# Six of the second layer's projections as seven block products each, over tokens that are normalized before they are turned

## The reference, cut to what matters

```python
def rmsnorm(x, g):
    y = xf * lax.rsqrt(jnp.mean(xf * xf, axis=-1, keepdims=True) + RMS_EPS)
    return (y * g.astype(jnp.float32)).astype(x.dtype)
...
    kv = (rmsnorm(x, g_kv) @ w_kv).reshape(b, t, N_DIL, 2, N_KV_B, HEAD_DIM)
...
    q = rmsnorm((h @ w_q).reshape(b, t, N_DIL, N_HEADS_B, HEAD_DIM), q_norm[:, None, :])
```

## Time and profile before

| | |
|---|---|
| median of 3 executions | 1359.59 us (1357.63 to 1359.62) |
| the profiled execution, its own time | 1362.34 us |
| its span in the trace | 1360.5 us |
| mean granted TensorE clock | 0.981 of 2.4 GHz |
| busy share of the span | PE 94%, DVE 47%, POOL 36%, ACT 24% |

### The profile page before, as it was taken

How to read it: one execution, slowest core, us unless ns; L and a number is a source line. 1 busy time by engine, 2 the same in 40 slices (tenths; PEclk the granted TensorE clock), 3 DMA queues, 4 the chain that set the end, 5 groups by cost and what they waited for, 6 DMA issues and landing times. The chain is left out here.

```text
span 1360.5 us, 20795 instructions
## 1 busy us (share of the span) xinstructions
PE 1275.2 (94%) x8580; PEld 894.0 (66%) x8580; DVE 639.7 (47%) x1018; ACT 331.5 (24%) x667; POOL 495.3 (36%) x415
## 2 busy tenths in 40 slices
PE   8999999999999988899999999999998999997786
PEld 6787887546566654458877877877755666664443
DVE  3578775524522211173559559558436572221114
ACT  2223322302122222140115015015005312222112
POOL 4466744101111111016876576576450111111101
PEclk8999999999999999899999999999999989999899
DMA  8446635577799999961113012013050899999996
GB/s 310 140 141 220 220 122 197 189 309 279 315 417 418 418 418 420 376 244 59 52 56 97 9 55 97 9 56 97 9 140 6 344 357 418 418 419 419 419 419 265
DMA packets 92768, 318.82 MB, mean 234 GB/s; under 512 B 32969, under 2 KB 45401, under 8 KB 66564
## 3 DMA queue, kind: packets, MB, share of 16 engines
q1 hardware_dynamic: 77956, 279.95, 52.9%
q0 software_dynamic: 13536, 33.29, 6.9%
q10 hardware_dynamic: 1184, 4.26, 0.8%
HBM read 300.19 MB, written 33.28 MB: 245 GB/s over the span
## 5 line engine op out<-in xcount | busy, mean ns | idle before, releaser
L2069 PE MATMUL ps<-slots 128*128 128x384 f32 x768 | 262.0, 495 | 1.1 <-DVE vo L2368 0.7
L2069 PEld LDWEIGHTS ps<-slots 128*128 128x128 f32 x768 | 203.0, 270 | 43.9 <-issue 3.2
L1215 PE MATMUL ps<-slots,oT 128*64 128x256 f32 x1216 | 160.9, 398 | 23.5 <-DMA slots<-in_w_up 21.9
L1215 PEld LDWEIGHTS ps<-slots,oT 128*64 128x64 f32 x1216 | 108.4, 144 | 72.6 <-issue 24.9
L1241 DVE TENSOR_TENSOR sg<-sg,ps 64x256 f32<-64x256 f32 x64 | 26.4, 413 | 242.9 <-ACT sg L1238 242.9
L1727 POOL DMA_INDIRECT xs<-xn_rows,idx x30 | 30.7, 1024 | 238.8 <-PE ps L1204 166.5
L1733 POOL DMA_INDIRECT y_rows<-ysb,idx x30 | 30.1, 1005 | 172.4 <-DVE ysb L1250 172.4
L1238 ACT ACTIVATE sg<-ps 64x256 f32<-64x256 f32 x64 | 24.4, 381 | 237.1 <-PE ps L1215 237.1
L1250 DVE COPY ysb<-ps 64x512 f32<-64x512 f32 x60 | 41.6, 694 | 85.8 <-PE ps L1233 79.9
L602 PE MATMUL ps<-xnT_a,wA 128*128 128x260 f32 (+1 forms) x320 | 76.9, 397 | 1.5 <-DVE xnT_a L866 1.4
L1233 PE MATMUL ps<-slots,hT 128*64 128x512 f32 x320 | 74.0, 598 | 4.2 <-issue 4.2
(11 more groups left out here) (338 smaller groups left out, 2335.5 us busy)
## 6 DMA issues: line engine op xcount, KB each, us to landing
slots<-in_w_up SPq DMA_DIRECT2D x42, 1024.0 KB, 28.0
slots<-in_w_down SPq DMA_DIRECT2D x40, 1024.0 KB, 29.0
slots<-in_w_gate SPq DMA_DIRECT2D x34, 1024.0 KB, 25.9
slots<-in_unit_weights_b SPq DMA_DIRECT2D x12, 1536.0 KB, 6.8
wA<-in_qkv_pairs_a SPq DMA_DIRECT2D x24, 512.0 KB, 3.8
apart<-in_w_gate SPq DMA_DIRECT2D x10, 1024.0 KB, 28.0
spare<-in_w_gate SPq DMA_DIRECT2D x8, 1024.0 KB, 27.8
scratch<-in_w_gate SPq DMA_DIRECT2D x8, 1024.0 KB, 28.5
```

The lines of the kernel that those rows point to most:

```text
L1215: last = nc.tensor.matmul(bank(q)[lo:lo + CAP, 0:FE], x[:, k, :], wt[:, k, :], start=(k == 0), stop=(k == KT - 1))
L2069: last = nc.tensor.matmul(bank(i % 2)[:, 0:UW], xT[:, kt, cols], wB[:, g, kt, :], start=(kt == 0), stop=(kt == KT - 1))
```

## The change

Four things change in `layer_b`:

1. **Tokens normalized at their turn.** `turn_x` becomes a matmul of the same stationary `x` with a diagonal matrix of `rs` instead of a transpose with the identity. So a tile's squares and `rs` come first. ACT makes the diagonal, in `gain_rows`. Evictions no longer multiply, and `rsr` with its two transfers is gone.
2. **Six units as seven block products.** Units 4, 5, 7, 8, 10, 11 (groups 1 and 2 of key heads 1 to 3) split tokens (residues 0, 1 and 2, 3), depth (4 and 4 blocks of 128) and columns (192 and 192) in halves, and form seven products of the Winograd kind. A product is 8 matmuls, 128 by 128 stationary and 128 by 192 moving. DVE makes the mixed tokens once (`mix_tokens`, 4 instructions) and the mixed weights per unit (`mix_weights`, 4 instructions of 768 elements per partition with both inputs in SBUF), and combines the products in `evict_mixed`. The sample tokens are part 7, as before.
3. **Raw blocks copied gapless.** ACT copies the unmixed token blocks once to places where their columns are neighbours. The last unit's third part reads `xT` with the stride instead.
4. **Norm weights by ScalarE.** `scale` goes from DVE to ACT (16 instructions a unit) for all units but unit 1. The parts of unit (j+1, 1) are also written one step earlier than its chunks were.

```diff
             NSTEP, NPART = sum(STEPS), 8
+            UQ, UH, HK = UW // 4, UW // 2, KT // 2
+            PARTS = ((0, 1), (2, 3), (4, 5), (6,), (7,))
+            def mixed(n):
+                return n > NDIL and n % NDIL > 0
...
                     def turn_x(t, rows):
-                        pe.wait_ge(s_cb, 3 * t + 3)
+                        pe.wait_ge(s_dg, t + 1)
...
-                            last = nc.tensor.transpose(dst[:, kt, 0:rows], x[0:rows, t, kt:D:KT], ident[0:rows, 0:rows])
+                            last = nc.tensor.matmul(dst[:, kt, 0:rows], x[0:rows, t, kt:D:KT], diag[0:rows, t % 2, 0:rows], start=True, stop=True)
...
+                    def mixed_part(n, part):
+                        g, i, w = n % NDIL, chunk0[n] + part, wB[:, n % NDIL]
+                        lower = copies[1] if n < NDIL * NKV - 1 else x_res[:, HK:KT, 0:2]
...
+                        elif part in (1, 3, 5):
+                            pe.wait_ge(s_wm, mixed0[n] + (2, 3, 4)[part // 2])
+                        pe.wait_ge(s_ev, i - 1)
...
+                            tokens = (copies[0], mix_x[1], lower, mix_x[2], mix_x[0], None, mix_x[3])[part]
...
+                        act.wait_ge(s_cb, 3 * t + 3)
+                        norm.square(act, t, junk)
+                        if t == 0:
+                            scale(0, 1, range(KT - 3, KT)).then_inc(s_ws, 1)
+                        act.wait_ge(norm.s_rstd, t + 1)
+                        nc.scalar.activation(diag[0:rows, t % 2, 0:rows], ident[0:rows, 0:rows], ACT.Copy, scale=rs[0:rows, t:t + 1]).then_inc(s_dg, 1)
                         act.wait_ge(s_xt, t + 1)
...
-                        norm.square(act, t, junk)
...
+                        turned(j, 0)
+                        if j < NKV - 1:
+                            scale_unit(j + 1, 0)
+                            scale_unit(j + 1, 1)
+                        turned(j, 1)
+                        if j < NKV - 1:
+                            scale_unit(j + 1, 2)
+                        turned(j, 2)
...
+                    def evict_mixed(j, g, part):
...
+                        if part == 0:
+                            room(j, g)
+                            V.tensor_copy(first_p, got).then_inc(s_ev, 1)
+                        elif part in (1, 3):
+                            dve.wait_ge(s_ev, i)
+                            V.tensor_tensor(early if part == 1 else late, first_p, got, ALU.add).then_inc(s_ev, 1)
...
+                            out, one, other = ((t1, b12, b11), (t2, b22, t1), (t3, b22, b12), (t2, b21, t2))[step]
+                            V.tensor_tensor(out, one, other, ALU.subtract).then_inc(s_wm, 1)
...
+                        parts(0, 1)
+                        soft(j, 2, 0)
                         if more:
-                            scale(j + 1, 1)
-                        ahead(1, 4)
-                        soft(j, 2, 0)
+                            mix_weights(j + 1, 1, (3,))
                         ahead(2, 0)
+                        parts(2)
                         soft(j, 2, 1)
                         far_max(j)
                         ahead(2, 1)
+                        parts(3, 4)
```

More of the change, by code:

```diff
@@ L2056, in project @@
                         n = 3 * j + g
-                        i = NCHUNK * n + c
+                        if mixed(n):
+                            for part in PARTS[c]:
+                                mixed_part(n, part)
+                            return
+                        i = chunk0[n] + c
                         if c == 0:
@@ L2073, in project @@
                                 pe.wait_ge(s_xc, NT)
-                            for kt in range(KT):
-                                for q in range(4):
-                                    last = nc.tensor.matmul(bank(i % 2)[32 * q:32 * q + DEC, 0:UQ], xT[:, kt, SEQ:TOK],
-                                                            wB[:, g, kt, UQ * q:UQ * q + UQ], start=(kt == 0), stop=(kt == KT - 1))
+                            last = sample_rows(i, g)
+                        last.then_inc(s_proj, 1)
@@ L2196, in _, with parts @@
                     project(0, 0, 4)
-                    for c in range(NCHUNK):
+                    for c in range(NT):
                         project(0, 1, c)
                     for j in range(NKV):
+                        more = j < NKV - 1
+                        def parts(*which):
+                            for part in which if more else ():
+                                mixed_part(3 * j + 4, part)
                         def ahead(u, c):
@@ L2239, in _ @@
                         ahead(1, 3)
+                        if more:
+                            ahead(1, 4)
+                            parts(0)
                         turn_back(j, 2, 0)
@@ L2255, in _ @@
                         weigh(j, 1)
-                        ahead(2, 3)
+                        parts(6)
                         turn_p(j, 3)
@@ L2260, in _ @@
                         weigh(j, 3)
-                        ahead(2, 4)
+                        parts(7)
                         turn_p(j, 5)
@@ new lines, in mix_tokens @@
+                    def mix_tokens(step):
+                        x11, x12, x21, x22 = [x_res[:, HK * i:HK * i + HK, c:c + 2] for c in (0, 2) for i in range(2)]
+                        out, one, other, op = ((0, x21, x22, ALU.add), (2, x11, x21, ALU.subtract), (1, mix_x[0], x11, ALU.subtract),
+                                               (3, x12, mix_x[1], ALU.subtract))[step]
+                        if step == 0:
+                            dve.wait_ge(s_xc, 4)
+                        elif step > 1:
+                            dve.wait_ge(s_mix, (1, 3)[step - 2])
+                        V.tensor_tensor(mix_x[out], one, other, op).then_inc(s_mix, 1)
@@ L2478, in _ @@
                     scale(0, 1)
-                    for c in range(2, NCHUNK):
+                    for c in range(2, NT):
                         evict(0, 0, c)
-                    for c in range(NCHUNK):
+                        if c == 2:
+                            for step in range(4):
+                                mix_tokens(step)
+                    for c in range(NT):
                         evict(0, 1, c)
-                        if c == 1:
-                            scale(0, 2)
                     for j in range(NKV):
@@ L2494, in ahead, with parts @@
                             elif more:
-                                evict(j + 1, u - 1, c)
+                                if u == 1:
+                                    evict(j + 1, 0, c)
                             elif (u, c) in GIVEN:
                                 out_b.add(dve, 0, GIVEN[u, c], at=0)
-                        if more:
-                            scale(j + 1, 0)
+                        def parts(*which):
+                            for part in which if more else ():
+                                evict_mixed(j + 1, 1, part)
                         ahead(0, 0)
+                        if j:
+                            mix_weights(j, 2, (3,))
                         ahead(0, 1)
@@ L2538, in _ @@
                         if more:
[L2539 to L2540 removed]
+                            mix_weights(j + 1, 2, (0, 1, 2))
+                        parts(6)
                         p_copy(j, 3)
```

177 lines of the change are left out of this document (131 added, 46 removed).

## The result

| | before | after |
|---|---|---|
| median of 4 executions | 1358.61 us | 1383.51 us (1383.21 to 1384.06) |
| ratio, 95% interval | | 1.0188 (1.0169 to 1.0207) |
| profiled execution, its span | 1362.3, 1360.5 us | 1383.2, 1381.4 us |
| PE busy, mean granted clock | 94%, 0.981 | 92%, 0.979 |

The forecast had the sign, but 1368.3 was too little by 15 us, and the range ended at 1382. All of the difference lies in the layer. I count from the moment at which DVE has tile 0 ready, 587.10 in the profile before and 583.15 after, since the stages ahead of it wander whatever is changed: over all kernels here that moment lies between 581.0 and 587.2. It is still one execution each. The differences in the head are good to about 1 us (see before_act_scale, and the part on tile 0's chain).

A forecast was written before the change was run, and what follows sets the result against it. PE, busy 94% of the span, was taken to set the time. Head +13.7, first halves -6 and second halves +1 gave +8.7 us: from the median 1359.6 to 1368.3 us, range 1355 to 1382.

The forecast's parts named there:

- The third step of `far_max`: Second halves: multiplying 16 maxima by -1, given no wait for POOL; the halves were forecast at +0.3 us each, +1 together.
- The walk: Second halves, both programs followed to the last `weigh`: 48.1 us after against 47.8 before, maxima out at 18.9.
- rival A: Second halves: `far_max`'s second step also waits for L2588, maxima at 22.6, +12.3 us; total 1379.6 us, chance 0.25.
- What a strided load costs: Turn in the head: each strided fp32 load takes 0.21 us, a turn 3.4 instead of 1.0, tiles 1 to 4 +9.7.
- Rival C: Turn: a strided load occupies the path no longer than a gapless one, 0.11 us; total 1354.8 us, chance 0.17.
- D: Seven-product units: gapless loads bind at 0.19 us, 21.3 a unit, no gain; about 1386 us, chance 0.04.
- Tile 0's chain: Head, from tile 0 ready through squares, `rs`, diagonal and turn to the first projection: +4.7 us.
- its sum: Head forecast: +4.7 for tile 0, +9.7 for the later turns, -0.7 for no `rsr`, together +13.7 us.
- Edit 4 at nothing, the mixing and the copies under PE work: Scaling on ACT costed at 0 us; `mix_tokens` and the raw copies taken to lie under PE work.
- First halves, -6: First halves of j = 1 to 3: gains of 1.9, 1.9 and 2.1 us, with PE waiting 1.0 at the fourth scores.
- Second halves without the exclusion: Second halves if `far_max` comes ahead of POOL's L2587: halves end at 46.6, -3.6 us together.
- B: Second halves: `far_max` comes ahead of POOL's L2587, -3.6 us together; total 1363.7 us, chance 0.15.

The follow-up runs named there:

- before_act_scale: Kernel before, with only the norm-weight scaling moved from DVE to ScalarE; ratio 0.9997 to the kernel before.
- neg_on_act: Changed kernel, but ScalarE instead of DVE multiplies the 16 maxima of `far_max` by -1; ratio 1.0104 to the kernel before.
- pool_holds: Changed kernel, but POOL holds its two large multiplications in three `front` calls until `far_max` has given the negated maxima; ratio 1.0073 to the kernel before.
- no_products: Changed kernel without the seven-product units and their copies, the six units projected in long-matmul chunks as before; ratio 1.0129 to the kernel before.

## Why the prediction was wrong, by its own steps

- **The third step of `far_max`.** This is what failed. The walk had the maxima out 18.9 behind the end of `ahead(1, 3)`, if the second instruction slips in ahead of L2588. It did slip in, 0.02 us ahead, and the first step ended where the walk put it (18.2 for 18.5). By these rows that question made no difference: had the second step waited for L2755 instead, the third would have followed it at once, and the maxima would have come as late. Behind the second step stands L2413, now L2567, which the walk took at its 0.17. I had written that a DVE instruction *with two SBUF inputs* waits for POOL's large ones, and so let a one-input instruction pass. It waited 3.41, and in all three second halves. The maxima came at 21.9, near rival A's 22.6 though by another instruction, and the halves cost 13.5 for its 12.3. neg_on_act shows this instruction's share (12.2 of the layer, and second halves of +1.3 for the forecast +1 without it), pool_holds the whole. (The Trainium skill, "SBUF — State Buffer", section "Who interferes with whom", names `tensor_scalar` among the instructions that can take both of DVE's port pairs and so shut GpSimd out or wait for it. The trace agrees, 3.41 us for 16 elements; I had read only its sentence on two inputs.) A single input alone does not make an instruction wait: L2555, a reduction, took its 1.22 while L2754 began beside it.
- **What a strided load costs.** Mechanism right, size off. 0.23 in place of 0.21, and the turn before was 0.88 and not 1.0 from its start to the next instruction's, so a turn is +2.8 and four are +11.2, where 9.7 stood. The 0.21 was the distance of the first two loads of a chunk. In the strided part of the last unit after, that is again 0.21, but 0.23 from the second load on. Rival C needed 0.11 and is out. The seven-product units' gapless loads hid under 0.163 and its last, strided part took 3.95 us for 2.76, so D is out too.
- **Tile 0's chain.** +4.7 forecast, +6.2 measured (first projection 10.10 behind tile 0, 3.85 before). The turn is 4.21 for 3.6, and L392 behind it, at the low clock, took 2.70 for 1.9 and ended later than the copy that I had on the path. The 1 to 2 us for the clock, which were kept out of the sum, came. Each of the two measured numbers has 1 us of its execution in it: pool_holds, neg_on_act and no_products have the same turns and show 9.2 for the 10.10, with 3.4 us at the low clock for 6.8, and before_act_scale shows 2.8 for the 3.85. The difference is hardly touched by that. The low clock came again behind the 8-token turn: L2091's 8 instructions took 4.44 for 2.85 (+1.6). Together the head is 4.3 over its sum.
- **Edit 4 at nothing, the mixing and the copies under PE work.** Right for edit 4 (before_act_scale). The mixing was hidden only by the long turns: with these mended PE waits 1.5 to 1.8.
- **First halves, -6.** Right: -2.0 each, and the fourth scores' wait is 0.85 for the forecast 1.0.
- **Second halves without the exclusion.** B's -1.2 each was right to 0.3, in pool_holds.

## What to carry to other kernels

When a walk meets an exclusion between two engines, list every instruction of both in the stretch and ask of each whether it is subject to it, by its kind and not only by its number of inputs (here a `tensor_scalar` with one input waited, a reduction with one did not); one of 16 elements can carry the whole price. Then ask whether the other engine can wait a moment: here 1.3 us of waiting on POOL bought 5.5 of PE's. And fit an edit that loads a strided stationary operand to the form whose spacing does not grow with the stride, transposes here, before counting what the new arithmetic saves.

## What the runs showed of the hardware that I had not expected

- The stride's price depends on the instruction and on the clock. At 2.4 GHz matmuls with 128 fp32 stationary columns eight elements apart stand 0.23 us apart and gapless ones 0.11; at 1.2 GHz it is 0.25 and 0.22. Transposes, one instruction each, stand 0.11 apart with and without the stride at 2.4 GHz. ScalarE takes 2.17 us for 1024 elements read with that stride and 1.15 without. (The Trainium skill, "SBUF — State Buffer", section "Door 1: The DMA port swizzle", says that each access which leaves a line of 16 bytes is penalized. The matmuls and ScalarE agree. So do the transposes' loads, 192 ns for 141, but not their time, 1.04 us for eight either way.)
- The exclusion works in both directions, but the power, as far as these runs show, only meets it at its start: it took 6.24 for 4.37 when it began just behind DVE's 2.0 us mixing, and neither lost anything when DVE's two-input instruction of 0.96 us began inside it. DVE's sum with one input in PSUM and ACT's instruction passed POOL's large ones unhindered (0.55 and 0.22, in neg_on_act).
- 3.6 us of filler on PE ahead of 3.9 us of idling did not keep the clock up behind them, and a wait of 2.6 us in the second halves of neg_on_act left it up where one of 3.9 did not.
